# Recurrence: the old state enters through two VectorE adds in place of two identity products

## The reference, cut to what matters

```python
per_dir.append((heads(decay), kd, kk * heads(a), g))
...
y = _rwkv7_scan(stack(rh, rh), stack(w_f, w_b), stack(k_f, k_b), stack(vh, vh),
                stack(-kk, -kk), stack(b_f, b_b)).swapaxes(0, 1)
```

## Time and profile before

| | us |
|---|---|
| median of three runs | 3095.57 |
| the profiled execution, its own time | 3098.44 |
| its span (first to last instruction) | 3096.6 |
| TensorE matmul busy in the span | 2859.8 (92%) |
| VectorE busy | 972.9 (31%) |
| ScalarE busy | 438.2 (14%) |
| GpSimd busy | 175.3 (6%) |
| granted TensorE clock, mean over the span | 0.955 |

### The profile page before, as it was taken

The page is one execution under the profiler, slowest core; times in us unless marked ns, Lnnn a source line. Parts: engine busy times, 40 slices in busy tenths (PEclk is TensorE's granted clock), DMA queues, the critical chain, the costliest instruction groups (busy, mean ns, idle before and its releaser), DMA issues. The chain is left out here.

```text
span 3096.6 us, 55478 instructions
## 1 busy us (share of the span) xinstructions
PE 2859.8 (92%) x24539; PEld 1691.2 (55%) x24539; DVE 972.9 (31%) x1999; ACT 438.2 (14%) x980; POOL 175.3 (6%) x210
## 2 busy tenths in 40 slices
PE   8999999699889899999979978869999999999998
PEld 6678988544477564455435547744343443434434
DVE  2422677438654336540024744330000000000001
ACT  1401100213332110000012231110010000000001
POOL 0000000000134000000000024100000000000000
PEclk9999999799999899988999989979999999999999
DMA  7244667231300226522213220049899899998995
GB/s 236 93 136 136 201 231 253 77 100 54 84 3 3 68 82 212 180 84 68 75 48 100 82 57 3 2 191 393 327 357 350 338 355 339 356 351 338 346 346 212
DMA packets 181992, 562.32 MB, mean 182 GB/s; under 512 B 28752, under 2 KB 41420, under 8 KB 165370
## 3 DMA queue, kind: packets, MB, share of 16 engines
q1 hardware_dynamic: 160675, 497.73, 44.9%
q0 software_dynamic: 13856, 53.11, 4.8%
q10 hardware_dynamic: 7223, 7.85, 0.9%
HBM read 557.43 MB, written 1.23 MB: 180 GB/s over the span
## 5 line engine op out<-in xcount | busy, mean ns | idle before, releaser
L1265 PE MATMUL bank<-normed,weight_ring 128*128 128x256 f32 (+2 forms) x2528 | 674.7, 428 | 13.3 <-PEq L2148 7.9
L1265 PEld LDWEIGHTS bank<-normed,weight_ring 128*128 128x128 f32 x2528 | 458.0, 192 | 221.7 <-issue 182.7
L2620 PE MATMUL bank<-weight_ring,work 128*32 128x384 f32 (+1 forms) x3072 | 310.5, 560 | 36.8 <-issue 35.7
L659 PE MATMUL bank<-normed,weight_ring 128*128 128x512 f32 (+1 forms) x704 | 281.2, 560 | 24.7 <-PEq L1360 24.7
L2620 PE MATMUL bank<-work 128*32 128x384 f32 (+1 forms) x3072 | 298.0, 540 | 0.0
L1265 PE MATMUL bank<-work,weight_ring 128*128 128x256 f32 (+2 forms) x928 | 285.4, 467 | 12.2 <-PEq L1231 12.2
L220 DVE SCALAR_TENSOR_TENSOR work<-work,small 128x512 f32<-128x512 f32 x336 | 237.6, 749 | 24.3 <-DMA work<-in_mod_w 17.7
L1265 PEld LDWEIGHTS bank<-work,weight_ring 128*128 128x128 f32 x928 | 177.3, 193 | 116.4 <-issue 102.0
L2620 PEld LDWEIGHTS bank<-weight_ring,work 128*32 128x32 f32 x3072 | 100.6, 113 | 235.7 <-issue 235.7
L659 PEld LDWEIGHTS bank<-normed,weight_ring 128*128 128x128 f32 x704 | 135.2, 193 | 169.5 <-issue 165.4
L2620 PEld LDWEIGHTS bank<-work 128*32 128x32 f32 x3072 | 97.4, 110 | 183.6 <-issue 183.6
(11 more groups left out here) (342 smaller groups left out, 2530.2 us busy)
## 6 DMA issues: line engine op xcount, KB each, us to landing
weight_ring<-in_moe_w_down SPq DMA_DIRECT2D x64, 1024.0 KB, 10.3
work<-in_mod_w POOLq DMA_DIRECT2D x48, 1024.0 KB, 6.8
work<-in_moe_w_down SPq DMA_DIRECT2D x48, 1024.0 KB, 10.8
weight_ring<-in_w_in SPq DMA_DIRECT2D x36, 1024.0 KB, 5.3
weight_ring<-in_moe_w_gate SPq DMA_DIRECT2D x32, 1024.0 KB, 5.7
work<-in_moe_w_gate SPq DMA_DIRECT2D x32, 1024.0 KB, 8.4
weight_ring<-in_moe_w_up SPq DMA_DIRECT2D x32, 1024.0 KB, 5.4
work<-in_moe_w_up SPq DMA_DIRECT2D x32, 1024.0 KB, 6.7
```

What stands on the lines that cost most here:

```text
L659: last = self.nc.tensor.matmul(self.bank(t)[:, 0:a.shape[-1]], tile[:, j * P:(j + 1) * P], a, start=k == 0, stop=k == DT - 1)
L1265: last = nc.tensor.matmul(banks(gi)[j][:, to], w[:, k, j * P:(j + 1) * P], a, start=k0 + k == 0, stop=k0 + k == total - 1)
L2620: last = nc.tensor.matmul(self.bank[3 * up + a][g * R:(g + 1) * R, 0:n], xg[:, k, a * R:(a + 1) * R], w[:, g * n:(g + 1) * n], start=k == ...
```

## The change

The two identity products of each step are gone. The first product of L517 into each bank now has `start=True`, and S holds only the chunk's own sum. In the state step VectorE first adds S (PSUM) to the state (SBUF), once per direction, and then multiplies the state by the decay, with all operands in SBUF. The second instruction on a direction waits for the first through a new semaphore, `state_carried`.

```diff
@@ scan_pe
             last.then_inc(self.dsum.sem, 1)
-            for d in range(2):
-                nc.tensor.matmul(S[d][:, 0:2 * P], self.pr.tab("ident"), self.state[:, 2 * d:2 * d + 2].rearrange("p f n -> p (f n)"),
-                                 start=True, stop=False)
             for f in range(2):
                 fc = slice(f * P, (f + 1) * P)
                 for d in range(2):
                     h, r = hf[d]
-                    nc.tensor.matmul(S[d][:, fc], btok[r, 2 * d + 1, fc], self.vtok[r, tile[d], fc], start=False, stop=False)
+                    nc.tensor.matmul(S[d][:, fc], btok[r, 2 * d + 1, fc], self.vtok[r, tile[d], fc], start=f == 0, stop=False)
@@ scan_dve
             dve.wait_ge(self.ssum.sem, self.ssum.at(n + 1))
+            for d in range(2):
+                both = self.state[:, 2 * d:2 * d + 2]
+                nc.vector.tensor_tensor(both, S[d][:, 0:2 * P].rearrange("p (f n) -> p f n", f=2), both, ALU.add).then_inc(self.carried.sem, 1)
             dve.wait_ge(self.dready.sem, self.dready.at(n + 1))
             for d in range(2):
-                last = nc.vector.tensor_tensor(self.state[:, 2 * d:2 * d + 2], S[d][:, 0:2 * P].rearrange("p (f n) -> p f n", f=2),
-                                               self.decay[:, c, 2 * d:2 * d + 2], ALU.mult)
+                both = self.state[:, 2 * d:2 * d + 2]
+                dve.wait_ge(self.carried.sem, self.carried.at(2 * n + d + 1))
+                last = nc.vector.tensor_tensor(both, both, self.decay[:, c, 2 * d:2 * d + 2], ALU.mult)
             last.then_inc(self.stepped.sem, 1)
```

More of the change, by code:

```diff
@@ L292, in __init__ @@
         self.ysum, self.ymoved, self.ssum, self.stepped = c("y_summed"), c("y_moved"), c("state_summed"), c("state_stepped")
-        self.dready = c("decay_ready")
+        self.dready, self.carried = c("decay_ready"), c("state_carried")
     def close(self):
@@ L299, in close @@
                      (self.umoved, 8), (self.ysum, 2 * (4 - self.first_out)), (self.ymoved, 2 * (4 - self.first_out)), (self.ssum, 8),
-                     (self.stepped, 9), (self.dready, 8)):
+                     (self.stepped, 9), (self.dready, 8), (self.carried, 16)):
             q.advance(n)
```

## The result

The changed kernel takes 3081.88 us (median of 5 runs, 3079.83 to 3085.15) against 3096.48 us (5 runs, 3094.32 to 3099.23): a ratio of 0.995 with a 95% interval of 0.9939 to 0.9962. It is faster by 14.6 us.

What follows compares the result with a forecast made beforehand. TensorE was taken as the main engine in the scans, with waits on other engines. 12.3 saved less 3.4 for VectorE and 3.2 for turns gave 5.7 us, so 3095.6 - 5.7 = 3089.9 us; range 3084.8 to 3098.

Steps and rivals of the forecast that it cites:

- The removed products: TensorE's identity products L511, four in each of 16 steps of the two scans: 12.3 us saved in sum.
- each odd step: Six odd steps under a solve (n = 1, 3, 5, twice): 1.06 us saved each, 6.4 us.
- bare step: Four steps without a solve (n = 6, 7, twice): 1.04 us saved each, 4.2 us.
- the even ones under a solve: Six even steps where L383 also waits for GpSimd's L481: 0.29 us saved each, 1.7 us.
- The added VectorE work: Two more VectorE instructions a step, 0.68 us, partly in idle time: 3.4 us lost in sum, without turns.
- The wait of L507 in step 7: TensorE's L507 waits for the state step from step 6 to 7: 0.9 us in place of 0.25.
- layer 1's part: VectorE's added work in layer 1's scan, including 0.65 us for each L439 without an output, 1.3 us.
- the doubtful term: Even steps under a solve: VectorE's SBUF multiply and GpSimd's L605 take turns, delaying L383; 3.2 us lost.
- Rival 1: No turns: the multiply gets in before L605 or beside it; 8.9 us saved, 3086.7 us; chance 0.29.
- The second failed step: With no transfer under way, what a scan saves should move all that follows by the same amount.
- The clock in the scans: Rival 2: the 1.57 us even-step wait lowers the clock; in all six, 4.5 us slower, 3100.1 us; chance 0.12.
- The products were not hidden: Rival 3 claimed products hidden in odd steps, only bare steps gaining: 2.4 us slower, 3098.0 us; chance 0.09.

Runs made afterwards that it cites:

- product_out: The kernel before with only the identity products removed, so the old state is not carried: 3081.28 us, ratio 0.9945.
- vector_only: The changed kernel with the identity products back beside the four VectorE instructions, so the state is added twice: 3223.94 us, ratio 1.0415, tokens going to other experts.
- big_neighbour: The changed kernel plus one GpSimd product of two 512-column SBUF operands ahead of the decays of odd steps 1, 3 and 5: 3089.52 us, one run.
- before_late: The kernel before with the products L507 issued twice in steps 1 and 3 of each layer: 3094.0 us, ratio 0.9993.
- before_shift1: The kernel before with the products L507 of step 1 issued twice: 3100.86 us, one run.
- before_shift3: The kernel before with the products L507 of step 1 issued four times: 3098.63 us, one run.
- level1_first: The changed kernel with GpSimd picking level 1 first and TensorE's wait for `xt_seeded` moved to the first L391: 3077.06 us, ratio 0.9936.
- after_third: A third, unchanged copy of the changed kernel, measured beside the three shifts of the kernel before: 3085.48 us, ratio 0.9961.

## Why the prediction was wrong in its size

**The removed products** were right: 12.3 us forecast, 12.7 measured by product_out. Set against before product by product, each odd step and each bare step gives 1.06 us (priced 1.06 and 1.04), and the even ones under a solve give 0.14 to 0.30 in layer 0 and 0.30, 0.30 and 0.59 in layer 1 (priced 0.29), with L481 as the new releaser and 0.31 more behind the last of these.

**The added VectorE work** was right as well: 3.4 forecast, 2.9 measured by vector_only, and that with the neighbour's cost in it. Two parts were off. The wait of L507 in step 7 is 1.13 in place of 0.9, because L579 started 0.88 after L574 and not two pitches of 0.34; in layer 1 the pitch is the expected one there, and I have no cause for these 0.2 us. And layer 1's part was too dear: some 2.1 expected without turns, and 1.8 measured.

**The first failed step is the doubtful term**, the turns between L579 and the four GpSimd decays: 3.2 us taken. Measured are 0.10 us a pair. In layer 0 that goes into the idle time; in layer 1 L436 is 0.38 late, and by L507 nothing is left of it. The even step's row shows it, and so does the sum 12.7 - 2.9 = 9.8. The error was in the row chosen. L427 stood beside one instruction of 512 columns and two operands and took 0.95 too long, and I carried that over as "each waits for the other's whole instruction" to four instructions of 128 columns and one operand. Which neighbour it is decides the cost: 0.85 beside the small ones, 1.60 beside the large one, both measured at the same place. Whether it is its columns, its operands or its operation that counts stays open. And the path was priced too dear as well: a late L383 was taken as lost in full, and in layer 0 of big_neighbour half of it came back at the next product. The Trainium skill (page SBUF — State Buffer, section on SBUF's two separate sides) says that the pair is held for the whole instruction. Big_neighbour agrees that a large one blocks. The four small ones disagree: by the profile the first L606 takes 0.85 us and starts 0.04 ahead of the first L579. By that rule L579 would have been held until its end, and it takes 0.42 all the same. Rival 1 of the prediction, no turns, is what happened; it gave 3086.7 us, 4.8 above the median.

**The second failed step** is that what follows the scans moves by the same amount. The scans gave 9.7 us (4.9 and 4.7, means of three profiles of after against two of before). Outside of them the means of three and two come to: between the scans 2.0 us less, of which the two L234 runs and the products between them make 3.8 and the rest of the stretch gives 1.8 back; from the second scan to the experts 1.1 more; the experts' stage 1.7 less, within what the same kernel varies by (1024.2 to 1027.2). The four sum to 12.3 us. That the L234 run is short is no property of the changed code: before_late, before_shift1 and before_shift3 have it with the old code, product_out and level1_first lack it though their scans are shorter still. What the kernels with a short run share is a clock that comes back 23.4 us or later behind layer 0's scan. The extra 1.1 us ahead of the experts are in most variants of either code. Of them 0.5 to 0.8 lie within 39 us behind layer 1's scan, where the clock is at full speed again 17.4 to 18.1 us after the scan's end in the three profiles of after and 16.5 and 16.6 in those of before; the rest I didn't place.

**How the 14.6 come about.** The forecast was a gain of 5.7 us. The scans gave 4.0 more, 3.2 of it the turns that didn't come; the stretches outside gave 2.6, and 2.3 of the medians' difference are in no profile. So the step that failed explains under half of the miss, and small errors in the scans another 0.8; the rest is luck of the clock and of the sample, and the two copies of the changed kernel came out nearer to the forecast, at 3084.7 and 3085.5 us.

**The rivals.** The clock in the scans stayed at 0.99, so a wait of 1.57 us in the even step didn't lower it. The products were not hidden: odd steps gained their 1.06.

**What stays open.** The medians of the three measurements give 14.6 us, 11.7 (against the copy of before) and 13.1 (against the 9 runs of before beside after_third); executions of one kernel spread by 4 to 11 us. The profiles account for 12.3. Whether there is a further microsecond or two the runs can't tell. Nor do they tell what sets the time at which the clock comes back behind a scan, with which the pattern of the L234 run goes.

## What to carry to other kernels

Price interference between two engines by a row in which the neighbour has the size and the operands of yours; a row with four times the columns and twice the operands gave a cost that was not there, and a small experiment at the place itself settles it. Where a gain is capped by a wait for another engine, look at that engine's order next: here GpSimd's first instruction was not the one TensorE wanted first, and two edits in order gave another 9.9 us in the scans. And a change of 0.3% can be given or taken by a stretch that no one edited, so compare the stretches and not only the total, and repeat the copy of either kernel.

## What the runs showed of the hardware

- VectorE's multiply of two SBUF operands (128x256, two in a row) takes 0.75 us with GpSimd idle, 0.85 beside GpSimd instructions of 128 columns and one operand and 1.60 beside one of 512 columns and two operands. Beside the small ones the first GpSimd instruction grew too, from 0.59 to 0.85; beside the large one the first multiply took 1.27 and ended 0.28 after it. The add that reads one operand from a bank kept 0.76 for two.
- A run of 96 one-column products with their weight loads takes 15.6 to 16.2 us or 17.8 to 18.4 us, at a mean granted clock of 0.65 or 0.57 (after and before). The same kernel gave the same pattern in each profile (two of before, three of after), and an edit that moves the run by less than a microsecond can change it (18.15 to 15.55 us from before to before_shift1). In all 14 profiles it is short where the clock came back 23.4 us or more behind the end of layer 0's scan, and long where it came back 23.1 us or less behind it.
- TensorE waits of 1.57 and 1.59 us left the clock up; after the 2.94 us in tile 0 of layer 0 and the 2.58 in that of layer 1 it fell. Taking that one wait away gave full speed to the products behind it, 1.15 in place of 1.55 us for 32.
- Where a VectorE instruction waits for the instruction before the last on its own engine, the pitch of 0.34 us mostly stays (the pair L579 starts 0.67 after L574), but in the bare step 6 of layer 0 it is 0.88, in after and in vector_only alike; in layer 1 it is 0.67 there.
